# The last two down groups of three quarters of a second feed-forward as one seven-block product, with the squares they need made on ScalarE

## What is computed

```
h = rms_norm(x, norm_mlp)                                   # 512 x 1024
x = x + jnp.square(jax.nn.relu(h @ w_up)) @ w_down          # 1024 -> 4096 -> 1024
```

## Time and profile before

| | |
|---|---|
| time, median of 3 runs | 1265.33 us (1264.65 to 1265.78) |
| the profiled execution, first to last instruction (span) | 1262.8 us |
| TensorE busy | 1240.3 us, 98% of the span, 11269 matmuls |
| VectorE, ScalarE, GpSimd busy | 765.1, 586.2, 398.5 us |
| mean granted TensorE clock | 0.999 |
| second feed-forward, from quarter 1's first matmul to quarter 2's | 1002.81 to 1087.38 us |

### The profile page before, as it was taken

The page is one execution under the profiler, slowest core; times in us unless marked ns, Lnnn a source line. Parts: engine busy times, 40 slices in busy tenths (PEclk is TensorE's granted clock), DMA queues, the critical chain, the costliest instruction groups (busy, mean ns, idle before and its releaser), DMA issues.

```text
span 1262.8 us, 26628 instructions
## 1 busy us (share of the span) xinstructions
PE 1240.3 (98%) x11269; PEld 1142.4 (90%) x11269; DVE 765.1 (61%) x1037; ACT 586.2 (46%) x1036; POOL 398.5 (32%) x314
## 2 busy tenths in 40 slices
PE   8999999999899999999999999999999999999998
PEld 7777798888899999999999997776899999999997
DVE  6678745555558529458377567434584494673863
ACT  5545535445455426337145453545443262461652
POOL 6022236223004236236253233000051362443520
PEclk9999999999999999999999999999999999999999
DMA  6223300000433323323324232112223233232331
GB/s 199 67 67 100 100 2 3 3 4 3 143 126 101 101 67 109 126 72 130 101 73 156 74 108 77 59 67 78 74 76 125 69 101 115 86 111 91 101 118 67
DMA packets 102076, 108.88 MB, mean 86 GB/s; under 512 B 1972, under 2 KB 97254, under 8 KB 101959
## 3 DMA queue, kind: packets, MB, share of 16 engines
q1 hardware_dynamic: 101878, 106.93, 26.9%
q0 software_dynamic: 80, 0.26, 0.1%
HBM read 105.08 MB, written 2.10 MB: 85 GB/s over the span
## 4 chain that ended last, share of the span: by engine, by line
PE 91%; DVE 4%; ACT 2%; issue 1%; POOL 1%; DVEq 0%; POOLq 0%; ACTq 0%
PE ps L556 11%; PE ps L558 11%; PE ps L557 11%; PE ps L647 6%; PE ps L648 6%; PE ps L649 6%; PE ps L520 4%; PE ps L522 4%; PE ps L521 4%; PE ps L607 2%; PE ps L609 2%; PE ps L608 1%; PE ps L1179 1%; PE ps L870 1%; PE ps L1181 1%
## 5 line engine op out<-in xcount | busy, mean ns | idle before, releaser
L556 PE MATMUL ps<-w_hi,a_hi 128*128 128x256 f32 x1024 | 286.1, 279 | 0.0
L557 PE MATMUL ps<-w_lo,a_hi 128*128 128x256 f32 x1024 | 285.8, 279 | 0.0
L558 PE MATMUL ps<-w_hi,a_lo 128*128 128x256 f32 x1024 | 285.8, 279 | 0.0
L556 PEld LDWEIGHTS ps<-w_hi,a_hi 128*128 128x128 f32 x1024 | 192.4, 188 | 0.1
L557 PEld LDWEIGHTS ps<-w_lo,a_hi 128*128 128x128 f32 x1024 | 192.4, 188 | 0.1
L558 PEld LDWEIGHTS ps<-w_hi,a_lo 128*128 128x128 f32 x1024 | 192.4, 188 | 0.0
L1911 DVE TENSOR_TENSOR w_lo<-w_raw,w_hi 128x2048 fp32r<-128x2048 f32 (+1 forms) x55 | 131.0, 2382 | 72.3 <-ACT w_hi L1269 72.0
L1269 ACT ACTIVATE w_hi<-w_raw 128x2048 fp32r<-128x2048 f32 (+1 forms) x55 | 104.4, 1899 | 133.1 <-PE ps L558 108.3
L2834 POOL TENSOR_TENSOR hsq<-tmp 128x512 f32<-128x512 f32 x64 | 94.9, 1498 | 88.9 <-ACT tmp L1381 62.3
L2017 DVE TENSOR_TENSOR w_lo<-w_raw,w_hi 128x1024 fp32r<-128x1024 f32 (+1 forms) x72 | 94.8, 1331 | 26.1 <-ACT w_hi L1342 25.9
L647 PE MATMUL ps<-th,w_hi 128*128 128x256 f32 x384 | 108.0, 281 | 0.4 <-ACT tmp L1367 0.4
(11 more groups left out here) (420 smaller groups left out, 3112.4 us busy)
## 6 DMA issues: line engine op xcount, KB each, us to landing
w_raw<-w_ffn_up_dram SPq DMA_DIRECT2D x16, 1024.0 KB, 5.7
w_raw<-w_ffn_down_dram SPq DMA_DIRECT2D x16, 1024.0 KB, 5.2
w_raw<-w_up_dram SPq DMA_DIRECT2D x16, 1024.0 KB, 5.6
w_raw<-w_down_dram SPq DMA_DIRECT2D x16, 1024.0 KB, 5.2
w_raw<-w_in_first_dram SPq DMA_DIRECT2D x12, 1024.0 KB, 5.3
w_raw<-w_out_dram SPq DMA_DIRECT2D x8, 1024.0 KB, 5.4
xn<-x_dram SPq DMA_DIRECT2D x8, 512.0 KB, 5.1
w_raw<-w_in_dram SPq DMA_DIRECT2D x4, 1024.0 KB, 6.4
```

Of the source, the lines that this page charges most:

```text
L556: mm(o, hi[:, hb + k, tok], whi, start=first and own and k == ks[0], stop=False, skip_group_check=True)
L557: mm(o, hi[:, hb + k, tok], wlo, start=False, stop=False, skip_group_check=True)
L558: m = mm(o, lo[:, hb + k, tok], whi, start=False, stop=last and k == ks[-1], skip_group_check=True)
```

## The change

In the second feed-forward (b = 1), for q = 0 to 2 (`paired`), down groups 2 and 3 (512 columns together) become one product in seven blocks, each of 2 x 4 x 3 = 24 matmuls of 256 columns. The blocks of the activations are even against odd hidden blocks and the first against the last 256 tokens. GpSimd makes the token sums T1 to T4 for each u (`sums_dt`) from the float32 squares, and the weight sums D1, D2, D3 (in place) and D4 of 128 x 1024 (`sums_down`). ScalarE and VectorE split four token sums and seven weight blocks. In all quarters of both feed-forwards the float32 square moves from GpSimd to ScalarE, directly behind `square_high`; in the second feed-forward it also waits until GpSimd has used what the buffer held (`dt_sum`). The buffers D4, dt_hi, dt_f32 and dt_lo lie over memory that is free then (delta, tmp, yT); D1 shares `hn_odd` with S1 and S2.

The diff, cut:

```diff
+        def paired(b, q):
+            return b == 1 and q < 3
...
         def block_free(b, q, u, n):
             g = group(b, q, u)
+            if u == 0 and b == 1:
+                return done(g - 2) + {A11: SUM3, A12: SUM3, SUM2: SUM4, SUM1: SUM4, SUM3: A22, SUM4: A22, A22: SUM1}[n] + 1
...
# SyncE, load_ffn
                         if q and u > 1:
                             sp.wait_ge(sm["s_sum"], 4 * seventh(b, q, u - 2) + 4)
+                        if u == 0 and q and paired(b, q - 1):
+                            sp.wait_ge(sm["d_sum"], 4 * q)
                         load(g + u, up[:, q * D + u * GW:q * D + (u + 1) * GW])
...
# TensorE
+            def seven_down(q):
...
+                pe.wait_ge(sm["db_lo"], down_at(q, A11))
+                one(A11, 0, True)
+                pe.wait_ge(sm["w_lo_ready"], g + 1)
+                one(A12, 1, True)
+                pe.wait_ge(sm["db_lo"], down_at(q, SUM2))
+                pe.wait_ge(sm["dt_lower"], 4 * q + 4)
+                pe.wait_ge(sm["tile_evacuated"], tile + 1)
+                one(SUM2, 0, False)
+                pe.wait_ge(sm["db_lo"], down_at(q, SUM1))
+                one(SUM1, 2, True)
+                pe.wait_ge(sm["db_lo"], down_at(q, SUM3))
+                pe.wait_ge(sm["tile_evacuated"], tile + 3)
+                one(SUM3, 0, False)
+                pe.wait_ge(sm["db_lo"], down_at(q, SUM4))
+                one(SUM4, 3, True)
+                pe.wait_ge(sm["w_lo_ready"], g + 2)
+                pe.wait_ge(sm["tile_evacuated"], tile + 6)
+                one(A22, 0, False)
...
-                    for c in range(1, 4 if q < 3 else 2):
+                    for c in range(1, 4 if q < 3 and not paired(b, q) else 2):
                         natural_group(g + c, tile + 2 * c, 0, a_hi, a_lo)
+                    if paired(b, q):
+                        seven_down(q)
...
# ScalarE
-            def square_high(u, j):
+            def square_high(b, q, u, j):
                 act.drain()
                 af(a_hi[:, 2 * u + j, :], tmp[:, 2 * (u % 2) + j, :], ACT.Square).then_inc(sm["a_ready"], 1)
+                act.wait_ge(sm["squared"], square_at(b, q, u) + j + 3)
+                summed = 4 * q + u if paired(b, q) else 12
+                if b == 1 and summed:
+                    act.wait_ge(sm["dt_sum"], summed)
+                af(hsq[:, j, :], tmp[:, 2 * (u % 2) + j, :], ACT.Square).then_inc(sm["square_f32"], 1)
...
                     split(g + 1)
+                    if paired(b, q):
+                        for t in (1, 0, 2, 3):
+                            upper_down_t(q, t)
+                        for x in (A11, A12, SUM2, SUM1, SUM3, SUM4, A22):
+                            upper_down(q, x)
+                        upper_a(b, q + 1, 0)
+                        upper_sum(b, q + 1, 0, SUM2)
+                        upper_sum(b, q + 1, 0, SUM1)
+                        continue
...
# VectorE
+            def seven_down(q, before_last, before_end):
+                lower_down(q, SUM2)
+                lower_down(q, SUM1)
+                add_product(q, A11, 0, 0, 0)
+                lower_down(q, SUM3)
+                dve.drain()
+                add_product(q, A12, 1, 0, 0)
+                lower_down(q, SUM4)
+                add_product(q, SUM2, 0, 1, 0)
+                dve.drain()
+                add_product(q, SUM1, 2, 1, 0)
+                add_product(q, SUM1, 2, 1, 1)
+                lower_down(q, A22)
+                dve.drain()
+                add_product(q, SUM3, 0, 1, 1)
+                before_last()
+                add_product(q, SUM4, 3, 1, 0)
+                before_end()
+                add_product(q, A22, 0, 0, 1)
...
# GpSimd
+            def sums_dt(q, u):
+                pool.wait_ge(sm["square_f32"], square_at(1, q, u) + 2)
+                low, high = slice(0, 2 * P), slice(2 * P, 4 * P)
+                t1, t2, t3, t4 = (dt_f32[:, n, u, :] for n in range(4))
+                g_.tensor_tensor(t1, hsq[:, 0, high], hsq[:, 0, low], ALU.subtract)
+                g_.tensor_tensor(t3, hsq[:, 1, high], hsq[:, 0, high], ALU.subtract)
+                pool.drain()
+                g_.tensor_tensor(t2, hsq[:, 1, high], t1, ALU.subtract)
+                pool.drain()
+                g_.tensor_tensor(t4, hsq[:, 1, low], t2, ALU.subtract).then_inc(sm["dt_sum"], 1)
...
                         if u < 3:
                             last_sum(b, q, u + 1)
-                        if u:
-                            square_f32(b, q, u - 1, 0)
-                            square_f32(b, q, u - 1, 1)
+                        if u and paired(b, q):
+                            sums_dt(q, u - 1)
                         if u < 2:
                             sums_s(b, q, u + 2)
-                    square_f32(b, q, 3, 0)
-                    square_f32(b, q, 3, 1)
+                    if paired(b, q):
+                        sums_dt(q, 3)
+                        sums_down(q)
```

More of the change, by code:

```diff
@@ L97, in program @@
         rstd = sb("rstd", [P, S])
+        with ExitStack() as s:
+            r = held(s)
+            D4 = r("D4", [P, KH, GW])
         delta = sb("delta", [P, S])
@@ L311, in done @@
         def done(g):
-            return 2 * g + 5 * sum(group(b, q, u) < g for b in range(2) for q in range(4) for u in seven(q))
+            return (2 * g + 5 * sum(group(b, q, u) < g for b in range(2) for q in range(4) for u in seven(q))
+                    + 3 * sum(group(1, q, 7) < g for q in range(3)))
         def block_free(b, q, u, n):
             g = group(b, q, u)
+            if u == 0 and b == 1:
+                return done(g - 2) + {A11: SUM3, A12: SUM3, SUM2: SUM4, SUM1: SUM4, SUM3: A22, SUM4: A22, A22: SUM1}[n] + 1
             if u == 0:
@@ L330, in block_at, with down_block, down_raw, down_at @@
             return 5 * seventh(b, q, u) + order.index(n) + 1
+        def paired(b, q):
+            return b == 1 and q < 3
+        def down_block(w, n):
+            at_ = {A11: 4, A12: 6, SUM2: 0, SUM1: 2, SUM3: 4, SUM4: 6, A22: 0}[n] * S
+            return w[:, at_:at_ + 2 * S].rearrange("q (k n) -> q k n", n=GW)
+        def down_raw(q, part):
+            j, k = divmod(part, 2)
+            return w_raw[:, group(1, q, 6 + j) % 2, k::2, :]
+        def down_at(q, n):
+            return 5 * q + (A11, SUM2, SUM1, SUM3, SUM4).index(n) + 1
+        def down_upper_t(n):
+            if n < 2:
+                return (h_hi, h_lo)[n][:, 0:KH, 2 * P:4 * P]
+            return dt_hi[:, n - 2]
         def raw(g, part):
@@ L676, in seven_products, with plain, one @@
                 one(A22, 0, False)
+            def seven_down(q):
+                g, tile = group(1, q, 6), tile_at(1, q, 6)
+                def plain(k, j, half):
+                    tok = rows(2 * j + half)
+                    return a_hi[:, 2 * k[0] + k[1], tok], a_lo[:, 2 * k[0] + k[1], tok]
+                def one(x, r, begin):
+                    o, whi, wlo = ps[:, 4 + r, :], down_block(block_hi, x), down_block(block_lo, x)
+                    for half in range(2):
+                        columns = slice(half * GW, (half + 1) * GW)
+                        for k in range(KH):
+                            if x == A11:
+                                hi, lo = plain((k, 0), 0, half)
+                            elif x == A12:
+                                hi, lo = plain((k, 1), 0, half)
+                            elif x == SUM4:
+                                hi, lo = plain((k, 1), 1, half)
+                            else:
+                                t = {SUM1: 0, SUM2: 1, SUM3: 2, A22: 3}[x]
+                                hi, lo = down_upper_t(t)[:, k, rows(half)], dt_lo[:, t, k, rows(half)]
+                            mm(o[:, columns], hi, whi[:, k, :], start=begin and half + k == 0, stop=False, skip_group_check=True)
+                            mm(o[:, columns], hi, wlo[:, k, :], start=False, stop=False, skip_group_check=True)
+                            m = mm(o[:, columns], lo, whi[:, k, :], start=False, stop=k == KH - 1, skip_group_check=True)
+                    m.then_inc(sm["mm_done"], 1)
+                pe.wait_ge(sm["db_lo"], down_at(q, A11))
[16 more added lines that the diff above has]
+                one(A22, 0, False)
@@ L2151, in ffn, with before_last, before_end @@
                     split(g + 1)
+                    if paired(b, q):
+                        lower_down_t(q, 1)
+                        lower_down_t(q, 0)
+                        add_rows(xn, tile, g, 0, cols_of(0))
+                        lower_down_t(q, 2)
+                        lower_down_t(q, 3)
+                        add_rows(xn, tile, g, 1, cols_of(0))
+                        lower_down(q, A11)
+                        lower_down(q, A12)
+                        for j in range(2):
+                            add_rows(xn, tile + 2, g + 1, j, cols_of(1))
+                        def before_last():
```

(6 more changed lines are left out.)

89 lines of the change are left out of this document (71 added, 18 removed).

## The result

The changed kernel takes **1281.58 us**, median of 4 runs (1280.9 to 1284.97), against 1265.05 for the kernel before in the same comparison. The ratio is 1.0131, 95% interval 1.0114 to 1.0147. It is slower, by 16.5 us; the prediction said 1262.9 and ended its range at 1268.0. The profiled execution of the changed kernel took 1281.77 us, with a span of 1279.9, 17.1 more than before's 1262.8. The granted clock over the span was 0.998.

A forecast was written before the change was run, and what follows sets the result against it. TensorE, busy 98% of the span, was taken as the bound. Terms -8.4 + 5.6 + 0.4 = -2.4 us took the span from 1262.8 to 1260.4; the median, 2.5 above, was forecast at 1262.9 us, range 1258.0 to 1268.0.

The forecast's parts named there:

- 72 matmuls, 8.4 us: Down parts of three quarters: 24 fewer matmuls each at 0.1167 us, 2.80 us per quarter, 8.4 us saved.
- Does the down product itself wait? I cost this part at nothing: Down parts: weights, sums and splits arrive in time; cost nothing, with 0.6 us of cover at the A11 add.
- 1.42 of 1024 columns: Down part: time taken for VectorE's low-part subtraction of 1024 columns, from a row of the kernel before.
- G: Time of TensorE's first down matmul in a quarter, from which the prediction counted the down part's times.
- the 1.79: VectorE subtraction time with GpSimd at work, against 0.68 us otherwise; read as 0.68 plus most of a GpSimd instruction.
- third rival: Down product waits: load, D sums and splits 3 us late in each of three quarters, 1271.9 us; chance 0.04.
- second rival: Each GpSimd instruction waits for a VectorE one: 4.75 us lost per quarter in two quarters, 1268.2 us; chance 0.17.
- The order on GpSimd: Up parts, quarters 1 and 2: token sums delay group 3's weight sums; TensorE stops 2.2 and 0.55 us, 5.6 in all.
- Squares on ScalarE elsewhere, 0.4 us: Quarters 1 to 3 of first, 3 of second feed-forward: added ScalarE squares cost 0.2 us each, 0.4 net.
- the 0.2 us of slack: Up part: copy 0 of group 2 ended at 1025.32, wanted by SUM2 at 1025.53.
- The 0.1 us for copy 2 of group 3: Up part: with ScalarE's added squares, this copy comes 0.1 us late for TensorE.
- 2 us at group 1: Cover for next quarter's group 1 weight sums: load lands at G + 42.0, sums wanted 4.7 us later.

The follow-up runs named there:

- e4: Changed kernel with the four down weight sums of each paired quarter moved from GpSimd to VectorE: 1273.09 us, ratio 1.0060.
- e7: Changed kernel with all added sums (token sums and down weight sums) on VectorE instead of GpSimd: 1267.33 us, ratio 1.0011.
- e2: Kernel before with only the float32 squares moved to ScalarE, down groups left as they were: 1270.48 us, ratio 1.0035.
- e5: Changed kernel with the float32 squares of the first feed-forward and of quarter 3 of the second back on GpSimd: 1280.66 us, ratio 1.0116.
- e11: e7 with ScalarE's copies out of PSUM waiting for the float32 square of two groups before instead of VectorE's low part: 1263.62 us, ratio 0.9984.
- e3: Changed kernel with each of GpSimd's four 128x1024 down weight sums issued as four pieces of 128x256: 1279.09 us, ratio 1.0103.

## Why the prediction was wrong

- **"72 matmuls, 8.4 us": right.** 11197 matmuls, and down parts of 42.3 us (e4) and 42.06 to 42.18 (e7) as soon as nothing holds them up.
- **"Does the down product itself wait? I cost this part at nothing": wrong, the largest error**, 10.8 us for 0. The step that failed is VectorE's low part at "1.42 of 1024 columns". Beside D1 to D4 it measured 6.65 / 2 and 6.15 / 2 us. So A11's low part came at G + 23.8, behind the end of the plain groups, and the A11 add ended at G + 31.2 in place of 27.4 (G is 961.20). e4, which takes GpSimd's sums away, shows that this is all of it but 1.0 us. The prediction had the price in its hands: it read the 1.79 as 0.68 and most of a GpSimd instruction of 1.29, and did not read the low parts beside D sums of 2.4 in the same way, which gives up to 3.6 for one (measured 2.8 to 3.4). The loads and D's own times were nearly right: D4 was done at G + 26.1, against G + 25. The third rival had the amount, 3 us per quarter, with the chance of 0.04, but as lateness of loads, sums and splits, and added to the forecast alone, not to the second rival.
- **"The order on GpSimd": mechanism right, size too small.** Token sums 1027.92 to 1032.10 are 4.2 us against the 3.8 taken; S1 took 2.26 in place of 1.3 to 1.5. TensorE's first stop was 3.1 us in both quarters against 2.2, the second 1.7 in quarter 2 against 0.55, and in quarter 1 a slower clock took some 1.5 us in its place (below). Together 10.3 us for 5.6, of which the squares on ScalarE alone are 1.5 (e2). The second rival's price, 4.75 per quarter, was the nearest: it had counted whole waits between the two engines.
- **"Squares on ScalarE elsewhere, 0.4 us": too small**, and partly of another cause. The first feed-forward lost 2.6 us, all of it the squares' (e5, e11): copy 0 of group 2 stood behind VectorE's low part, and the 0.2 us of slack turned into stops of 0.3 to 0.6 us. (The 0.1 us for copy 2 of group 3 was right; it is 0.15.) Of quarter 3's 1.3 us, 0.6 was theirs (e2). The other 0.7 comes with the pairing, and its cause stays open: group 1's weight sums, which had "2 us at group 1" of cover, begin 0.3 us into the up part, but in e4 they begin later still and the up part takes 40.14.
- **The sum.** -8.4 + 5.6 + 0.4 was -2.4; measured -8.4 + 10.8 + 10.3 + 2.6 + 1.3 + 0.5 = +17.1. The three costs had been weighed as rivals of one another, where they add: with the third rival's 9 in addition to the second's +2.9, the text's own prices give +11.9. A small slip lies in the 2.5 us between span and median: an execution's time lies 1.7 to 1.9 us above its own span (1281.77 and 1279.9), and the rest was spread among the executions of the kernel before.

Still open: how much of e3's loss is its clock; what holds quarter 3 up by 0.7 us; and why a stop of 3.2 us brought the clock down in quarter 1 and not in quarter 2 of the same execution.

## What to carry to other kernels

Before work is put on GpSimd, look at which VectorE instructions run at that moment, not at GpSimd's busy share: each two-input VectorE operation on SBUF can cost the length of the GpSimd instruction beside it, and a longer one costs more. Here the same 20 sums per quarter made the kernel 15 us slower on a GpSimd that was 31% busy than on a VectorE that was 63% busy (shares of the changed kernel; e7 against it, 1.0011 and 1.0131). And where one change adds several costs in different stretches, add them up; rivals with a chance each are for cases that exclude one another.
